# Passing expert tokens and results through row scratches in HBM instead of one-hot matmuls

## What is computed

```python
def moe_ffn(h, router_w, wg, wu, wd):
    t = h.reshape(-1, D)                       # 256 x 1024
    logits = t @ router_w                      # 256 x 8
    vals, idx = lax.top_k(logits, TOP_K)       # TOP_K = 2
    probs = jax.nn.softmax(vals, axis=-1)
    gates = jnp.sum(jax.nn.one_hot(idx, N_EXPERTS) * probs[..., None], axis=1)
    y = jnp.zeros(t.shape)
    for e in range(N_EXPERTS):
        y = y + gates[:, e:e + 1] * swiglu(t, wg[e], wu[e], wd[e])   # D_FF = 3584
    return y
```

## Time and profile before

| | us |
|---|---|
| median of 3 runs | 1556.64 (1555.27 to 1559.91) |
| span of the profiled execution | 1554.6 |
| its TensorE busy | 1505.7 |
| its VectorE busy | 1218.9 |
| its ScalarE busy | 1018.9 |
| start of the expert items (first gather) | 528.5 |

### The profile page before, as it was taken

The page is one execution under the profiler, slowest core; times in us unless marked ns, Lnnn a source line. Parts: engine busy times, 40 slices in busy tenths (PEclk is TensorE's granted clock), DMA queues, the critical chain, the costliest instruction groups (busy, mean ns, idle before and its releaser), DMA issues.

```text
span 1554.6 us, 22425 instructions
## 1 busy us (share of the span) xinstructions
PE 1505.7 (97%) x7892; PEld 1284.1 (83%) x7892; DVE 1218.9 (78%) x1381; ACT 1018.9 (66%) x1209; POOL 21.7 (1%) x45
## 2 busy tenths in 40 slices
PE   7998999998999799999999999999999999999997
PEld 7987999997998688888878888888888887888885
DVE  7755545545676798889889889989888988888997
ACT  6644434444654477777777777777777777777775
POOL 0001000001000100000000000000000000000000
PEclk9969999999997799999999999999999999999999
DMA  9604554554532199989989989989998998998993
GB/s 369 244 7 169 190 190 163 198 185 159 184 136 96 68 351 375 356 320 371 360 320 364 372 308 367 372 317 355 368 346 325 372 351 327 361 370 313 368 360 138
DMA packets 63069, 437.80 MB, mean 282 GB/s; under 512 B 9008, under 2 KB 9136, under 8 KB 10288
## 3 DMA queue, kind: packets, MB, share of 16 engines
q1 hardware_dynamic: 60048, 432.98, 74.0%
q10 hardware_dynamic: 2976, 4.20, 0.9%
HBM read 436.10 MB, written 1.05 MB: 281 GB/s over the span
## 4 chain that ended last, share of the span: by engine, by line
PE 96%; DVE 2%; ACT 1%; issue 0%; DMA 0%; POOL 0%; SPq 0%; DVEq 0%; ACTq 0%
PE psum L414 29%; PE psum L416 29%; PE psum L415 29%; PE psum L664 2%; PE psum L679 2%; PE psum L727 2%; PE psum L548 1%; ACT lru_b L776 0%; PE psum L500 0%; PE psum L559 0%; PE psum L558 0%; DVE xs L1082 0%; DMA con<-consts 0%; DVE hT_lo L991 0%; PE psum L557 0%
## 5 line engine op out<-in xcount | busy, mean ns | idle before, releaser
L980 DVE TENSOR_TENSOR w_lo<-ring,w_hi 128x1024 fp32r<-128x1024 f32 x819 | 956.2, 1220 | 130.3 <-ACT w_hi L763 124.2
L763 ACT ACTIVATE w_hi<-ring 128x1024 fp32r<-128x1024 f32 x819 | 817.8, 1053 | 145.6 <-PE psum L416 145.5
L414 PE MATMUL psum<-w_hi,hT_hi 128*128 128x512 f32 (+1 forms) x1152 | 438.9, 381 | 0.0
L416 PE MATMUL psum<-w_hi,hT_lo 128*128 128x512 f32 (+1 forms) x1152 | 429.9, 373 | 0.0
L415 PE MATMUL psum<-w_lo,hT_hi 128*128 128x512 f32 (+1 forms) x1152 | 429.4, 373 | 0.0
L416 PEld LDWEIGHTS psum<-w_hi,hT_lo 128*128 128x128 f32 x1152 | 217.6, 189 | 38.9
L415 PEld LDWEIGHTS psum<-w_lo,hT_hi 128*128 128x128 f32 x1152 | 218.0, 189 | 38.0 <-issue 1.7
L414 PEld LDWEIGHTS psum<-w_hi,hT_hi 128*128 128x128 f32 x1152 | 218.0, 189 | 37.7 <-DVE w_lo L980 1.7
L414 PE MATMUL psum<-w_hi,act_hi 128*128 128x512 f32 x560 | 222.3, 397 | 0.0
L415 PE MATMUL psum<-w_lo,act_hi 128*128 128x512 f32 x560 | 221.5, 396 | 0.0
L416 PE MATMUL psum<-w_hi,act_lo 128*128 128x512 f32 x560 | 221.5, 396 | 0.0
(11 more groups left out here) (209 smaller groups left out, 860.4 us busy)
## 6 DMA issues: line engine op xcount, KB each, us to landing
ring<-moe_gate SPq DMA_DIRECT2D x114, 1024.0 KB, 5.2
ring<-moe_up SPq DMA_DIRECT2D x114, 1024.0 KB, 6.4
ring<-moe_down SPq DMA_DIRECT2D x112, 1024.0 KB, 6.5
ring<-in_units SPq DMA_DIRECT2D x20, 1024.0 KB, 8.1
ring<-dense_gate SPq DMA_DIRECT2D x14, 1024.0 KB, 4.8
ring<-dense_up SPq DMA_DIRECT2D x14, 1024.0 KB, 4.8
ring<-dense_down SPq DMA_DIRECT2D x14, 1024.0 KB, 4.8
ring<-out_units SPq DMA_DIRECT2D x8, 1024.0 KB, 5.7
```

The source lines that it names most:

```text
L414: pe.matmul(dst, s_hi, m_hi, start=start, stop=False)
L416: return pe.matmul(dst, s_lo, m_hi, start=False, stop=stop)
L763: act.activation(w_hi[:, h % AHEAD, :], ring[:, n % RING, (h % 2) * HCOLS:(h % 2 + 1) * HCOLS], ACT.Copy).then_inc(hi_ready, 1)
L980: dve.tensor_tensor(w_lo[:, h % AHEAD, :], ring[:, (h // 2) % RING, (h % 2) * HCOLS:(h % 2 + 1) * HCOLS], w_hi[:, h % AHEAD, :].bitcast(F3 ...
```

## The change

Two scratches in HBM are added: x_rows with 12 blocks of 128 rows (one for each possible item, and one more), and y_rows with 11. Rows are 1024 float32 (4 KB).

- GpSimd clears lru_g after the norm ahead of the dense FFN; during the dense FFN ScalarE's queue writes it over all of x_rows and over the three extra blocks of y_rows.
- The router works out for each token two row numbers (dest_i) and two gates (pair_gate) in place of item_slot, item_gate and the gate matrices. GpSimd's queue then scatters hn to x_rows with four indirect DMAs (two choices by two halves of the tokens).
- Item 0 still gathers with one-hot matmuls (into banks 7 and 3). For each later item SyncE loads the 128 rows of the next item into hn[:, 0, :], behind the load of unit gate 4, and TensorE transposes them with 8 matmuls before the second unit of down 5 (`turn_rows`). Both halves are split then.
- At an item's end ScalarE copies the result to ye and stores it to y_rows on its own queue. The combine, pick_g, its transposes and the adds are gone.
- After the last item, when all stores have landed, GpSimd's queue gathers two rows for each token with four indirect DMAs, VectorE weights and adds them (into qk), and the norm goes on from there.

```diff
@@ sync
                     sync.dma_start(ring[:, (NPRE + n) % RING, :],
                                    source_e[kind][expert, 2 * c + i]).then_inc(unit_loaded[(NPRE + n) % RING], 16)
+                    if (kind, c, i) == ("gate", 4, 0):
+                        sync.wait_ge(scattered, 16 * 2 * TT)
+                        sync.wait_ge(gathered, item * 2 + 2)
+                        sync.dma_start(rows_in, x_items[item + 1]).then_inc(rows_loaded, 16)
@@ gpsimd
+                    if (layer, which) == (0, PRE_FFN):
+                        pool.memset(flat(lru_g), 0.0).then_inc(rows_zero, 1)
+                    if (layer, which) == (1, PRE_FFN):
+                        pool.wait_ge(y_stored, 32)
+                        pool.wait_ge(dest_ready, 1)
+                        for j in range(2):
+                            for tt in range(TT):
+                                pool.indirect_dma_start(
+                                    out=x_rows, out_offset=bass.IndirectOffsetOnAxis(ap=dest_i[:, j, tt:tt + 1], axis=0),
+                                    in_=hn[:, tt, :], in_offset=None).then_inc(scattered, 16)
+                        pool.wait_ge(y_all, 1)
+                        for tt in range(TT):
+                            for j in range(2):
+                                pool.indirect_dma_start(
+                                    out=y_pair[j][:, tt, :], out_offset=None, in_=y_rows,
+                                    in_offset=bass.IndirectOffsetOnAxis(ap=dest_i[:, j, tt:tt + 1], axis=0)
+                                ).then_inc(y_gathered[tt], 16)
@@ tensor
+            def turn_rows(b, bank):
+                for k in range(4):
+                    mm = pe.transpose(ps[bank][:, k * C:(k + 1) * C], rows_in[:, (4 * b + k) * P:(4 * b + k + 1) * P],
+                                      ident)
+                return mm
...
-                    if (kind, c, i) == ("gate", 1, 0):
-                        pe.wait_ge(comb_added, item * 4 + 1)
...
-                        pe.wait_ge(silu_ready, item * ENC + (NCH + ENC))
-                        pe.wait_ge(pick_ready, item + 2)
-                        gather(0)
+                        pe.wait_ge(rows_loaded, item * 16 + 16)
+                        turn_rows(0, 7).then_inc(gathered, 1)
+                        turn_rows(1, 3).then_inc(gathered, 1)
                         turn_prod(ENC - 1)
...
-                    if (kind, c, i) == ("down", 0, 1):
-                        pe.wait_ge(pick_g_ready, item + 1)
-                        for tt in range(TT):
-                            mm = pe.transpose(ps[7][:, tt * P:(tt + 1) * P], pick_g[:, tt, :], ident)
-                        mm.then_inc(pick_tr, 1)
-                gather(1)
-                pe.wait_ge(pick_gT_ready, item + 1)
-                pe.wait_ge(ye_ready, item + 1)
-                for o, bank in enumerate((2, 3, 6, 7)):
-                    tt, half = o // 2, o % 2
-                    pe.matmul(ps[bank], pick_gT[:, tt * P:(tt + 1) * P],
-                              ye[:, half * 512:(half + 1) * 512], start=True, stop=True).then_inc(comb_ready, 1)
@@ scalar
+                if (kind, c) == ("gate", 2):
+                    act.wait_ge(rows_zero, 1)
+                    act.dma_start(x_rows.rearrange("(m c) d -> c m d", c=C),
+                                  flat(lru_g).unsqueeze(1).to_broadcast([P, NITEM + 1, D])).then_inc(y_stored, 16)
+                    act.dma_start(y_rows[EXPERTS * C:, :].rearrange("(m c) d -> c m d", c=C),
+                                  flat(lru_g).unsqueeze(1).to_broadcast([P, NEXTRA, D])).then_inc(y_stored, 16)
...
                     if (kind, c, i) == ("down", ENC - 1, 0):
-                        tok_hi(item * 2 + 2, (0,))
-                    if (kind, c, i) == ("down", 0, 1):
-                        act.wait_ge(pick_tr, item + 1)
-                        act.activation(pick_gT, ps[7][:, 0:T], ACT.Copy).then_inc(pick_gT_ready, 1)
+                        tok_hi(item * 2 + 2)
                     if (kind, c, i) == ("down", ENC - 1, 1):
                         act.wait_ge(half_done, item * (2 * NEU) + 2 * (NPRE + NEU))
+                        act.wait_ge(y_stored, item * 16 + 32)
                         act.activation(ye, psum[:, 4:6, :].rearrange("p a b -> p (a b)"),
                                        ACT.Copy).then_inc(ye_ready, 1)
+                        act.wait_ge(ye_ready, item + 1)
+                        act.dma_start(y_items[item], ye).then_inc(y_stored, 16)
...
+            act.wait_ge(y_stored, extras * 16 + 16 * (2 + EXPERTS))
+            act.activation(junk[:, 0:1], eps[:, :], ACT.Copy).then_inc(y_all, 1)
@@ vector
-                for o, bank in enumerate((2, 3, 6, 7)):
-                    tt, half = o // 2, o % 2
-                    dst = y_sum[:, tt, half * 512:(half + 1) * 512]
-                    dve.wait_ge(comb_ready, item * 4 + (o + 1))
-                    dve.tensor_tensor(dst, dst, ps[bank], ALU.add).then_inc(comb_added, 1)
+            for tt in range(TT):
+                dve.wait_ge(y_gathered[tt], 16 * 2)
+                link(dve.tensor_scalar(qk[:, tt, :], qk[:, tt, :], pair_gate[:, 0, tt:tt + 1], None, ALU.mult))
+                dve.scalar_tensor_tensor(out=qk[:, tt, :], in0=hn[:, tt, :], scalar=pair_gate[:, 1, tt:tt + 1],
+                                         in1=qk[:, tt, :], op0=ALU.mult, op1=ALU.add).then_inc(y_ready, 1)
+            dve.wait_ge(y_ready, TT)
```

More of the change, by code:

```diff
@@ L328, in build @@
         pick_ready = sem("pick_ready")
-        pick_g_ready = sem("pick_g_ready")
-        pick_tr = sem("pick_tr")
-        pick_gT_ready = sem("pick_gT_ready")
         gathered = sem("gathered")
+        rows_zero = sem("rows_zero")
+        y_stored = sem("y_stored")
+        dest_ready = sem("dest_ready")
+        scattered = sem("scattered")
+        rows_loaded = sem("rows_loaded")
+        y_all = sem("y_all")
+        y_gathered = [sem(f"y_gathered{i}") for i in range(TT)]
+        y_ready = sem("y_ready")
         tok_hi_ready = sem("tok_hi_ready")
@@ L657, in _, with gather @@
                       start=False, stop=True).then_inc(slots_mm, 1)
-            def gather(b):
+            def gather(b, bank):
                 for k in range(4):
                     for tt in range(TT):
-                        mm = pe.matmul(ps[b][:, k * C:(k + 1) * C],
+                        mm = pe.matmul(ps[bank][:, k * C:(k + 1) * C],
                                        hn[:, tt, (4 * b + k) * P:(4 * b + k + 1) * P], pick[:, tt, :],
@@ L824, in mixer @@
                     keep_up(first + i + 1)
+                if layer == 1:
+                    act.wait_ge(y_stored, 32)
                 for i in range(2):
@@ L920, in _, with tok_hi @@
             act.activation(top[:, 3, :], top[:, 2, :], ACT.Exp).then_inc(exp_diff, 1)
-            def tok_hi(first, banks=(0, 1)):
-                for b in banks:
+            def tok_hi(first):
+                for b, bank in enumerate((7, 3)):
                     act.wait_ge(gathered, first + (b + 1))
-                    act.activation(hT_hi[:, 4 * b:4 * b + 4, 0:C], ps[b].rearrange("p (k c) -> p k c", k=4),
+                    act.activation(hT_hi[:, 4 * b:4 * b + 4, 0:C], ps[bank].rearrange("p (k c) -> p k c", k=4),
                                    ACT.Copy).then_inc(tok_hi_ready, 1)
@@ L1283, in _, with tok_lo @@
             link(dve.tensor_scalar(slot[:, :, :], slot[:, :, :], -1.0, None, ALU.add))
[L1284 to L1297, removed]
+            for tt in range(TT):
+                ins = dve.tensor_scalar(pick[:, tt, :], cc("iota", 0, C), slot[:, tt, 0:1], None, ALU.is_equal)
+            ins.then_inc(pick_ready, 1)
+            def tok_lo(first):
+                for b, bank in enumerate((7, 3)):
                     dve.wait_ge(tok_hi_ready, first + (b + 1))
-                    minus(hT_lo[:, 4 * b:4 * b + 4, 0:C], ps[b].rearrange("p (k c) -> p k c", k=4),
+                    minus(hT_lo[:, 4 * b:4 * b + 4, 0:C], ps[bank].rearrange("p (k c) -> p k c", k=4),
                           hT_hi[:, 4 * b:4 * b + 4, 0:C]).then_inc(tok_ready, 1)
@@ L1320, in _ @@
             dve.tensor_copy(extra_i[:, :], extra_f[:, :]).then_inc(routed, 1)
[L1322 to L1326, removed]
-                link(dve.tensor_reduce(item_slot[:, tt, EXPERTS:NITEM], cand_work[:, 0, :, :], AX_X, ALU.add))
+            per_token = [P, TT, EXPERTS]
@@ new lines, in _ @@
+            link(dve.scalar_tensor_tensor(out=row_gap[:, :], in0=cand[:, 2, :], scalar=float(C), in1=cc("row_gap"),
+                                          op0=ALU.mult, op1=ALU.add))
+            link(dve.scalar_tensor_tensor(out=row_f[:, :, :], in0=slot[:, :, :], scalar=float(C),
+                                          in1=row_gap[:, :].unsqueeze(1).to_broadcast(per_token),
+                                          op0=ALU.is_ge, op1=ALU.mult))
```

(12 more changed lines are left out.)

68 lines of the change are left out of this document (29 added, 39 removed).

## The result

The changed kernel takes 1522.37 us (median of 4 runs, 1519.24 to 1524.51) beside 1557.14 us for the kernel before on the same chip: a ratio of 0.9764, with a 95% interval of 0.9746 to 0.9783. The forecast was 1518.4 us in a range of 1510 to 1536. The profiled span went from 1554.6 to 1522.3 us.

What follows compares the result with a forecast made beforehand. The prediction took TensorE's instruction list to bound each expert item. Saving 45.2 us there and adding 7.0 at the end gave −38.2: 1554.6 − 38.2 + 2.0 (runs over profiled span) = 1518.4 us, range 1510 to 1536.

Steps and rivals of the forecast that it cites:

- TensorE's list in an item: Expert items: gathers, combine and pick transposes go, eight row transposes come; 6.27 us saved in each of items 0 to 6.
- The splits' lead: Item change: half 5 of w_lo is ready 2.7 us before TensorE wants it, down from 8.3; nothing booked.
- rival 2: Item changes: splits come late, TensorE stalls about 2 us an item, 1534 us in all; chance 0.09.
- DMA: Expert items: traffic rises from 349 to 376 GB/s, under a limit taken as 424; nothing booked.
- Rival 1: Expert items: DMA becomes the bound; limit 368 GB/s gives 1538 us, chance 0.08; limit 351 gives 1583, chance 0.03.
- The front: Ahead of the experts: zero fill, GpSimd memset and scatters cost nothing; routing chain's shortening is worth nothing.
- The end: After the last down matmul: 23.2 us instead of 16.2, so 7.0 longer.
- G: Kernel end: time of the four row gathers, taken as 8.0 us, between 5 and 34.
- weighting of the last half: Kernel end, after the row gathers: weighting 1.2 + 1.3 us and a link, 2.6 us.
- store and handover: Kernel end, ahead of the row gathers: handover 0.2 us and the store 2.6 us to landing.
- Rival 3: Kernel end: the four gathers make it slower, from G = 46 us up; in small pieces 1668 us; chance 0.05.

Runs made afterwards that it cites:

- act_late1: Changed kernel with one extra 128x1024 ScalarE copy behind the y copy of each item; 1519.28 us, item 119.70 us.
- act_late4: Changed kernel with four extra 128x1024 ScalarE copies behind the y copy of each item; 1545.26 us, item 122.15 us.
- loads6: Changed kernel with six more 512 KB loads per item on SyncE's queue, read by nothing; 1527.37 us, item 119.70 us.
- plain_end: Changed kernel with the four indirect end gathers replaced by plain SyncE loads of fixed y_rows blocks (wrong result); 1521.01 us, ratio 0.9754 to the kernel before.

## Why the prediction was right, and where it was off

**TensorE's list in an item.** Right. 6.35 us saved, 6.27 predicted; the row transposes took 0.87 us for 0.88. That the saving came in full needed both halves of the change together, which the prediction did not see: it priced gather(1) at 1.79 us as if it stood for itself. Where the combine remains, its removal gives, by the sum above, only 1.79 − 1.59 = 0.2 us.

**The splits' lead.** Right in mechanism and size for half 5: 2.6 us, 2.7 predicted. The smallest is half 7's 2.0 us, because the table load comes between; this was the fear of rival 2, and the lead took it. `act_late1` and `act_late4` show that rival 2 is a true mechanism, and that its cost begins between 1.1 and 4.3 us of delay, at about 2 by the trace.

**DMA.** Right: 376 GB/s predicted and measured. Rival 1, in both its forms, falls with `loads6`. The ring loads' landing rose from 5.2 to 6.5 us to 6.6 to 7.1, and the row load and the y store landed in 7.5 and 6.7 us (DMA issues of the changed kernel):

```profile
ring<-moe_up SPq DMA_DIRECT2D x114, 1024.0 KB, 7.1
...
x_rows<-lru_g ACTq DMA_DIRECT2D x1, 6144.0 KB, 31.9
hn<-x_rows SPq DMA_DIRECT2D x8, 512.0 KB, 7.5
y_rows<-lru_d ACTq DMA_DIRECT2D x8, 512.0 KB, 6.7
```

**The front.** The zero fill, the GpSimd memset (0.95 us on GpSimd, waited for by nobody) and the scatters (0.95 to 1.20 us an issue) were booked at nothing. The traces bear this out: the dense FFN, beside which fill and memset run, is as long with them as without, 249.61 us. What the prediction missed is that a sum made against one profiled execution carries that execution's clock: the fronts of twelve profiles lie between 527.1 and 536.2 us, and 528.5 was an early one. Middle and end together give −45.5 + 8.2 = −37.2 us; the medians of the two kernels differ by 34.8 us. In the second set of runs they differ by 1559.61 − 1522.28 = 37.3 us, so the 2.4 us between are not a fixed cost of the change; both fit the spread of the fronts.

**The end.** This is the term that was mis-sized: 24.4 us for 23.2. G, the four row gathers, took 9.8 us where 8.0 was taken from xs<-x. `plain_end` divides the error: 8.2 of the 9.8 us come without any indirect DMA, so the estimate was right within 0.2 us for plain loads, and what lacked was a term for the indirect path by GpSimd. The weighting of the last half took 2.1 us for 2.6; store and handover 3.3 for 3.0. The sum itself was added up 0.2 us too high: its terms without G give 15.0 and not 15.2. By the Trainium skill's formula (DMA: Bandwidth & Descriptors, section Anatomy of one DMA) the four would take 3.2 us each, an estimate from the page's figures. The stretch of 9.8 us is shorter than four of these in series, 12.8, since issue and transfer of neighbours overlap, as the issues 1.25 us apart show. Rival 3, with its 46 us, has nothing for it.

## What to carry to other kernels

When a matmul leaves the path, look at what ran under it on other engines: the same exchange of the gathers for row transposes was worth 2.7 us an item where no combine followed, and 1.1 us where one did and the result's copy had hidden behind a gather, and parts of a change measured alone need not add up. A DMA share near 1 doesn't say that bandwidth is used up; add loads that nobody reads, and see when the period grows. Work moved from a loop to the kernel's bare end costs its full length there; peel the last round and put it behind that, here for another 9.5 us.

## What the runs showed of the hardware

- The same program's front varied by 6 us and more (mean granted clock 0.83 and 0.87 over the same 810 matmuls), while the item period repeated to 0.01 us.
- One core loaded 403 GB/s from HBM over 500 us without any wait of TensorE, and 413 GB/s, 417 in single items, when the loads held it up.
- An indirect DMA of 128 rows of 4 KB took GpSimd 0.94 to 1.44 us an issue at the idle end, 1.25 us from start to start after the first, and 1.75 to 1.96 us in the middle of an item, 2.05 to 2.25 from start to start, with VectorE and the ring at work. Which of the two makes it dearer was not tried.
- Four loads of 512 KB at the idle end took 8.2 us from first issue to last landing as plain DMAs from SyncE, and 9.8 us as indirect DMAs from GpSimd.
